# A two-block network in float32 on one core: the residual's second column half transposed without TensorE at two places

## What is computed

```python
for layer in range(DEPTH):                       # DEPTH = 2
    hn = rms_norm(h, mix_norm[layer])
    mixed = rg_lru_block(hn, ...) if layer == 0 else stick_breaking_attention(hn, ...)
    h = h + mixed
    h = h + swiglu_ffn(rms_norm(h, ffn_norm[layer]), ffn_w_in[layer], ffn_w_out[layer])
...
def swiglu_ffn(x, w_in, w_out):                  # 1024 -> 2 x 2816 -> 1024
    gu = jnp.einsum("bsd,df->bsf", x, w_in)
    h = jax.nn.silu(gu[..., :D_FF]) * gu[..., D_FF:]
    return jnp.einsum("bsf,fd->bsd", h, w_out)
```

## Time and profile before

| what | value |
|---|---|
| runs, us | 811.69, 810.04, 811.88 (median 811.69) |
| profiled execution, us | 809.93, of which its span 807.8 |
| PE busy | 802.0 us, 99% of the span |
| PEld busy | 695.2 us, 86% |
| DVE busy | 594.1 us, 74% |
| ACT busy | 533.9 us, 66% |
| POOL busy | 108.7 us, 13% |
| HBM read | 145.94 MB, 184 GB/s over the span with what is written |

### The profile page before, as it was taken

One profiled execution on the slowest core, in us unless ns is written; L12 is line 12 of the kernel. 1 busy time (PEld: TensorE's weight loads), 2 busy tenths in 40 slices (PEclk: granted clock), 3 DMA queues, 4 the chain that ended last, 5 costly groups with the idle time before them and its releaser, 6 DMA issues.

```text
span 807.8 us, 11976 instructions
## 1 busy us (share of the span) xinstructions
PE 802.0 (99%) x4482; PEld 695.2 (86%) x4482; DVE 594.1 (74%) x841; ACT 533.9 (66%) x867; POOL 108.7 (13%) x198
## 2 busy tenths in 40 slices
PE   9999999999999999999999999999999999999998
PEld 8999788888888899887888888888989899888887
DVE  6998886666655579987766666556867689998764
ACT  6887477677656557656766777737664857677432
POOL 0000023444402000000044444202100000000000
PEclk9999999999999999999999999999999999999999
DMA  8964697666565564436676666656464454553511
GB/s 276 324 195 130 224 285 242 198 198 207 186 203 185 157 183 150 143 104 185 209 252 189 183 201 192 192 193 194 159 192 134 154 186 129 173 175 127 184 69 53
DMA packets 119057, 147.79 MB, mean 183 GB/s; under 512 B 7079, under 2 KB 89816, under 8 KB 118872
## 3 DMA queue, kind: packets, MB, share of 16 engines
q1 hardware_dynamic: 117767, 145.43, 57.0%
q10 hardware_dynamic: 1232, 1.59, 0.6%
HBM read 145.94 MB, written 2.63 MB: 184 GB/s over the span
## 4 chain that ended last, share of the span: by engine, by line
PE 98%; DVE 1%; DMA 1%; ACT 0%; issue 0%; SPq 0%; DVEq 0%
PE bank L558 22%; PE bank L560 22%; PE bank L559 22%; PE bank L483 6%; PE bank L484 5%; PE bank L485 5%; PE bank L523 3%; PE bank L525 1%; PE bank L490 1%; PE bank L491 1%; PE bank L492 1%; PE bank L585 1%; PE bank L940 1%; PE bank L817 1%; PE bank L800 1%; DMA const<-in_consts 1%
## 5 line engine op out<-in xcount | busy, mean ns | idle before, releaser
L1728 DVE TENSOR_TENSOR wlo<-raw,whi 128x1024 fp32r<-128x1024 f32 (+1 forms) x268 | 315.9, 1218 | 57.4 <-ACT whi L1141 56.5
L1141 ACT ACTIVATE whi<-raw 128x1024 fp32r<-128x1024 f32 (+1 forms) x260 | 258.5, 1045 | 82.6 <-PE bank L560 60.9
L558 PE MATMUL bank<-whi,xboth 128*128 128x512 f32 x464 | 182.0, 392 | 0.4
L560 PE MATMUL bank<-whi,xboth 128*128 128x512 f32 x464 | 180.7, 389 | 0.0
L559 PE MATMUL bank<-wlo,xboth 128*128 128x512 f32 x464 | 180.6, 389 | 0.0
L1109 POOL COPY xg<-sq 32x128 f32<-32x128 f32 x176 | 96.6, 549 | 381.9 <-DVE sq L2077 375.4
L558 PEld LDWEIGHTS bank<-whi,xboth 128*128 128x128 f32 x464 | 87.1, 188 | 19.0 <-issue 1.1
L560 PEld LDWEIGHTS bank<-whi,xboth 128*128 128x128 f32 x464 | 87.1, 188 | 18.4
L559 PEld LDWEIGHTS bank<-wlo,xboth 128*128 128x128 f32 x464 | 87.1, 188 | 17.7
L483 PE MATMUL bank<-xboth,whi 128*128 128x256 f32 x352 | 100.8, 286 | 0.2 <-DVE wlo L1728 0.2
L485 PE MATMUL bank<-xboth,wlo 128*128 128x256 f32 x352 | 99.6, 283 | 0.0
(11 more groups left out here) (359 smaller groups left out, 1250.0 us busy)
## 6 DMA issues: line engine op xcount, KB each, us to landing
raw<-in_ffn_w_in SPq DMA_DIRECT2D x176, 256.0 KB, 3.6
raw<-in_w_in SPq DMA_DIRECT2D x48, 512.0 KB, 4.5
raw<-in_ffn_w_out SPq DMA_DIRECT2D x44, 512.0 KB, 4.1
raw<-in_attn_w_qkv SPq DMA_DIRECT2D x24, 512.0 KB, 4.6
raw<-in_lru_w_in SPq DMA_DIRECT2D x14, 512.0 KB, 6.5
raw<-in_lru_w_out SPq DMA_DIRECT2D x8, 512.0 KB, 4.3
raw<-in_attn_w_o SPq DMA_DIRECT2D x8, 512.0 KB, 4.8
raw<-in_w_out SPq DMA_DIRECT2D x8, 512.0 KB, 4.3
```

The costliest lines, as they stand in the source:

```text
L558: nc.tensor.matmul(dst, hi, wh, start=start, stop=False)
L560: return nc.tensor.matmul(dst, lo, wh, start=False, stop=stop)
L1141: nc.scalar.activation(whi[:, c % RING, part], raw[:, c % RAWS, part], ACT.Copy).then_inc(hi_done, 1)
L1728: nc.vector.tensor_tensor(wlo[:, c % RING, part], raw[:, c % RAWS, part], whi[:, c % RING, part].bitcast(F32), ALU.subtract).then_inc(lo_d ...
```

## The change

At both places the second column half (j = 2, 3 of norms 1 and 3) is no longer transposed by TensorE. Behind the addition to `h`, VectorE transposes it in 32x32 blocks (`x_turn`), and GpSimd and ScalarE carry the blocks to their partitions with eight copies each (`x_moves`); `norm_hi` and `norm_lo` then read `x_part` in SBUF where they read a PSUM bank. `late_transposes` goes out of `ffn`; it stays in the projections behind norms 2, 4 and 5. The odd norms have buffers of their own (12 and 16 KB into the arena). The tables `XT_BLOCKS` and `XT_BANKS` number the waits, and two increments that stood for transposes that TensorE did not do go away.

```diff
@@ -108,6 +108,13 @@
 X_BANKS = (6, 7, 4, 5)
+
+
+XT_BLOCKS = {(1, 1): 1, (2, 0): 2, (3, 1): 3, (4, 0): 4}
+
+
+XT_BANKS = {key: n + 1 for n, key in enumerate(
+    (xn, j) for xn in range(1, 6) for j in range(4) if (xn, j // 2) not in XT_BLOCKS)}
@@ -200,8 +207,8 @@
-        x_blocks = over("x_blocks", 44, [P, 4, 4, 2, 32])
-        x_part = over("x_part", 48, [P, 4, S])
+        x_blocks = [over(f"x_blocks{n}", kb, [P, 4, 4, 2, 32]) for n, kb in enumerate((44, 12))]
+        x_part = [over(f"x_part{n}", kb, [P, 4, S]) for n, kb in enumerate((48, 16))]
@@ -755,8 +762,6 @@
                     last.then_inc(chunk_done, 1)
-                    if p == 0:
-                        late_transposes(xn, ready, count)
@@ -775,12 +780,9 @@
                     last.then_inc(chunk_done, 1)
-                    if c == 7:
-                        pe.sem_inc(xt_mm, 1)
-                        pe.sem_inc(xt_mm, 1)
@@ -1097,7 +1098,18 @@
         def _(pool):
 
+            def x_moves(xn, half):
+
+                pool.wait_ge(xt_blocks, XT_BLOCKS[xn, half])
+                for i in range(2):
+                    rows = slice(32 * i, 32 * i + 32)
+                    for f in range(4):
+                        dst = x_part[xn % 2][32 * f:32 * f + 32].rearrange("p k (a n) -> p k a n", n=P)
+                        last = nc.gpsimd.tensor_copy(dst[:, :, :, rows], x_blocks[xn % 2][rows, :, f])
+                last.then_inc(xt_pool, 1)
+
             for layer in range(2):
+                x_moves(1 + 2 * layer, 1)
                 for q in range(FFN_PAIRS):
...
-                pool.wait_ge(xt_blocks, layer + 1)
...
+                x_moves(2 + 2 * layer, 0)
@@ -1160,15 +1166,29 @@
+            def x_moves(xn, half):
+
+                act.wait_ge(xt_blocks, XT_BLOCKS[xn, half])
+                for i in range(2, 4):
+                    rows = slice(32 * i, 32 * i + 32)
+                    for f in range(4):
+                        dst = x_part[xn % 2][32 * f:32 * f + 32].rearrange("p k (a n) -> p k a n", n=P)
+                        last = nc.scalar.activation(dst[:, :, :, rows], x_blocks[xn % 2][rows, :, f], ACT.Copy)
+                last.then_inc(xt_act, 1)
+
             def norm_hi(xn, j):
                 if xn == 0 and j == 0:
                     act.wait_ge(first_t, 1)
                 elif xn == 0:
                     act.wait_ge(chunk_done, j + 1)
+                elif (xn, j // 2) in XT_BLOCKS:
+                    act.wait_ge(xt_pool, XT_BLOCKS[xn, j // 2])
+                    act.wait_ge(xt_act, XT_BLOCKS[xn, j // 2])
                 else:
-                    act.wait_ge(xt_mm, 4 * (xn - 1) + j + 1)
-                if xn in (2, 4) and j < 2:
-                    src = [x_part[:, 2 * j:2 * j + 2, :].rearrange("p m n -> p (m n)")] * 2
+                    act.wait_ge(xt_mm, XT_BANKS[xn, j])
+                if (xn, j // 2) in XT_BLOCKS:
+                    k = 2 * (j % 2)
+                    src = [x_part[xn % 2][:, k:k + 2, :].rearrange("p m n -> p (m n)")] * 2
@@ -1359,6 +1379,7 @@
                 norm_square(xn, 0)
                 act.wait_ge(banks_read, b0 + 4 + 4)
                 norm_square(xn, 1)
+                x_moves(xn, 1)
                 norm_hi(xn, 2)
                 norm_hi(xn, 3)
@@ -1822,9 +1836,17 @@
+            def x_turn(xn, half):
+
+                cols = slice(half * WIDE, (half + 1) * WIDE)
+                nc.vector.transpose(x_blocks[xn % 2][:, :, :, :, :].rearrange("p k f a n -> p a (k f) n"),
+                                    h[:, :, cols].rearrange("p a (b n) -> p a b n", n=32)).then_inc(xt_blocks, 1)
+
             def norm_end(name, xn):
 
                 residual_wide(name, 1)
+                dve.wait_ge(banks_read, STAGES[name][2] + 8)
+                x_turn(xn, 1)
                 ahead(STAGES[name][0] + 3)
                 norm_sum(xn)
                 norm_lo(xn, 2)
```

More of the change, by code:

```diff
@@ L737, in _, with ffn @@
             outputs_wide("lru_out", yhi, ylo, y_lo, 1)
-            def ffn(layer, ready, count):
+            def ffn(layer):
                 c0, _, b0 = STAGES[f"ffn_in{layer}"]
@@ L777, in ffn @@
                     last.then_inc(chunk_done, 1)
-                    if c == 7:
-                        pe.sem_inc(xt_mm, 1)
-                        pe.sem_inc(xt_mm, 1)
             pe.wait_ge(p_lo, 1)
-            ffn(0, banks_read, STAGES["lru_out"][2] + 4 + 4)
+            ffn(0)
             c0, _, b0 = STAGES["qkv"]
@@ L852, in _ @@
                         after=4 if g == 1 else 2)
-            c0a, _, b0a = STAGES["attn_out"]
             o_h = ohi[:, :, :].rearrange("p a (b n) -> p (a b) n", n=S)
@@ L861, in _ @@
                           (2, 2): lambda: weight_transposes(GROUPS - 1), (3, 1): lambda: weighted_values(GROUPS - 1)})
-            ffn(1, banks_read, b0a + 4 + 4)
+            ffn(1)
             c0, _, b0 = STAGES["mix_in"]
@@ L1423, in ffn @@
                     if c == 7:
[L1424 to L1430, removed]
+                        x_moves(xn + 1, 0)
                         if layer:
@@ L1435, in ffn @@
                     if c == 8:
-                        act.wait_ge(xt_pool, layer + 1)
-                        act.wait_ge(xt_act, layer + 1)
                         norm_hi(xn + 1, 0)
@@ L2145, in ffn @@
                         dve.wait_ge(acc_read, 4 * layer + 2)
-                        nc.vector.transpose(x_blocks[:, :, :, :, :].rearrange("p k f a n -> p a (k f) n"),
-                                            h[:, :, 0:WIDE].rearrange("p a (b n) -> p a b n", n=32)).then_inc(xt_blocks, 1)
+                        x_turn(xn + 1, 0)
                     if c == 8:
@@ L2260, in final_norm @@
             def final_norm():
-                dve.wait_ge(xt_mm, 16)
+                dve.wait_ge(xt_mm, XT_BANKS[4, 3])
                 for a in range(2):
```

## The result

The changed kernel took 815.8 us as the median of seven executions (814.06 to 817.59); beside it the kernel before had a median of 810.11 (seven executions, lowest 810.02). The ratio is 1.0064 with an interval of 1.0054 to 1.0074: slower, by 0.6%. The profiled execution took 816.06 us, its span is 814.2, and the mean granted clock over it is 0.998.

What follows compares the result with a forecast made beforehand. The prediction took TensorE, busy for 802.0 of 807.8 us, to bound the kernel. Later starts of chunk p = 2, +2.5 and +1.5 us with the transposes' gain included, made +4.0 on a mean of 810.9: 814.9 us, range 811.7 to 817.7.

Steps and rivals of the forecast that it cites:

- The bound: Whole kernel: TensorE sets the time; work taken off it is gained, any wait of it lost in full.
- Step 1: Chunk p = 1: TensorE waits 0.74 us for `wlo` in the first layer, not at all in the second.
- Step 2: Chunk p = 2: starts late behind GpSimd's copies, +2.5 us at the first place, +1.5 at the second.
- What was costed at nothing: Later load into the freed `raw` slot (cover about 7 us), removed `xt_mm` increments, new buffers: no cost.
- Rival 1: Both places: GpSimd's copies are not slowed, ScalarE's end last; +1.8 us in all, 812.7; chance 0.18.
- Rival 2: Chunk p = 2 ready in time at both places, only the gain stays: 1.8 us less, 809.1; chance 0.04.
- Rival 4: The change does nothing at one of the places; given no chance.
- Rival 3: Behind the new waits the clock falls, one chunk per place at 1.2 GHz: 10.9 us more, 825.8; chance 0.05.
- The sum: Both places, gain and p = 1 wait included: +2.5 + 1.5 = +4.0 us, giving 814.9 us; chance 0.70.

Runs made afterwards that it cites:

- four additions: Kernel before, with four unneeded 128x1024 additions on VectorE ahead of `wlo` of chunk p = 2 at both places: 817.75 us, 1.0091.
- three additions: Kernel before, with three unneeded 128x1024 additions on VectorE ahead of `wlo` of chunk p = 2 at both places: 813.22 us, 1.0042.
- filled with matmuls: Changed kernel plus nine unread 128x512 matmuls on TensorE ahead of chunk p = 2 in both layers: 814.05 us, the second time 814.14.
- the three recut ones: Changed kernel recut: half-size copies, second place only, 811.31 us; copies on VectorE and ScalarE, splits around them, ten and six 810.14, eight and eight 809.15.
- eight and eight copies: Changed kernel with GpSimd moving nothing, VectorE and ScalarE eight copies each, splits put around the copies by halves: 809.15 us, 0.9991.

## Why the prediction was right, and where its sum was short

**The bound.** That TensorE's time is the kernel's held: each delay reached the end in full. The two starts of p = 2 are late by 4.2 us in sum, and the executions at full clock are 4.0 and 4.2 us over before.

**Step 1** (p = 1). Forecast: a wait of 0.74 us at the first place and none at the second. Measured: from 100.60 to 101.59 is 0.99, 0.76 over the step of 0.23, and none at the second. The profile names no cause for this wait (`issue`), but the first half of this row of VectorE, the first part of `wlo`, ends at 100.31 + 1.26 = 101.57:

```profile
100.31 2.52 DVE L1741 TENSOR_TENSOR wlo<-raw,whi 128x1024 fp32r<-128x1024 f32 x2
```

**Step 2** (p = 2). Forecast +2.5 and +1.5 us, measured +2.57 and +1.64. The hand-overs, the halves of each split and the order of the engines came out within 0.1 us. The price it rests on, GpSimd's 5.26 us from norm 4, was exact, and so was the reading of it as two long copies: in the changed kernel

```profile
L1108 POOL COPY a_x_part<-a_x_blocks x2: 1297/1298/1300, 100.4 to 101.8; 32x256 f32<-32x256 f32 x2
```

are the two beside `wlo`, and the six behind them took 0.395 us; where the transposition stands behind the subtractions, all eight took 0.392:

```profile
L1108 POOL COPY a_x_part<-a_x_blocks x8: 387/392/398, 104.2 to 107.3; 32x256 f32<-32x256 f32 x8
```

The Trainium skill, in "SBUF — State Buffer" (Who interferes with whom), says that a VectorE instruction with two SBUF inputs contends with a GpSimd instruction that reads SBUF, and calls the shared ports an exclusive lock. The trace agrees: one copy is held for each subtraction, by 0.9 us each.

**What was costed at nothing** stayed at nothing: no other new wait of TensorE is in the list, so the later load into the freed `raw` slot was covered.

**Rival 1** (ScalarE's copies last) fell: ScalarE waited 1.33 us for GpSimd. **Rival 2** (the waits vanish) fell as well; the kernel without copies shows what it would have given, -1.2 us. **Rival 4** fell: both places changed.

**Rival 3 is the step that was mis-sized,** and its own sign, a granted clock under 1.00 behind a gap, is in the profile. It was put as "one chunk of 5.46 us at each place", 10.9 us more, with a chance of 0.05 on the ground that 1.1 us of standing still had left the clock at full. The clock does fall: in 10 of 12 executions of the changed kernel, each with the mean clock of one fall. But it falls for about eight matmuls only, 1.7 us, and then comes back while TensorE works on. A cost of 1.7 us with a high chance was taken for one of 10.9 with a low one. The reason given for the small chance did not carry. The 1.1 us of the earlier trace rows stand ahead of TensorE's very first matmul, which starts at 1.05, so they say nothing of a clock behind work (kernel before):

```profile
1.05 4.63 PE L649 MATMUL bank<-rs 128*128 128x128 f32 x20 [1.05 <-DVE rs L1866]
```

And the length counts: the kernels with waits of up to 1.3 us kept the clock, those with about 2.4 or more lost it in 22 of 30 executions. The page "TensorE: Matmul & The Clock Gate" (HAM oscillation) of the Trainium skill was cited there for the fall; the trace agrees that there is one (0.50 in the windows), not that the whole chunk passes at the lower level.

**The sum.** Forecast +4.0 us, on executions at full clock +4.0 to +4.2, with one fall +5.8. The chain was right, by its mechanism and by its size. The forecast time of 814.9 came 0.9 us short of the 815.8 measured and within its range, and that it came so near is in part luck, since two errors partly cancel: 1.7 us of clock were left out, and the base of 810.9, the mean of four executions, was 0.8 above the 810.1 that the kernel before had as a median beside it. Of the chances, slower by over 0.3% had 0.75.

## What to carry to other kernels

Where one engine is busy for 99% of the span, price a unit of its work by the step between starts there, not by durations, and ask of every operation taken off it how many hand-overs take its place: here 0.9 us of transposes gave way to a chain over three engines that let TensorE stand for 2.4 us. When such an engine begins to stand still, count the clock in as well, and read it in windows of a few us around the gap, since a page of 20 us slices hides a fall of 3 us. If the bounding engine must wait for over 2 us, matmuls that nothing needs can keep the clock up (here 1.7 us), but it is better to shorten the wait: with the copies off GpSimd, the splits put around them and both sets of copies ending together, the kernel became 5 us faster here than the changed one is at full clock.

## What the runs showed of the hardware that was not expected

**The clock's fall behind a wait is partial and not certain.** Executions with a fall among all, by what TensorE did ahead of p = 2:

| kernels | gap between starts, us | executions with mean clock 0.998 or less |
|---|---|---|
| changed (twice), one place only (two kernels), transposition behind, four additions | 2.7 to 4.0 | 22 of 30 |
| three additions | 1.7 | 0 of 5 |
| filled with matmuls (twice) | 0.8, behind the filling | 0 of 10 |
| without copies, the three recut ones | up to 1.7 | 0 of 44 |
| before | none | 0 of 60 |

By kernel: one wait per execution 4 of 10, the changed kernel with its two 10 of 12, the transposition behind (gaps of 4.0 and 3.1 us) 4 of 4, and four additions 4 of 4, though their gaps of 2.8 us are hardly longer than the 2.8 and 2.7 of the changed kernel. Why one execution falls and the next doesn't was not tried; nor is it settled why the changed kernel's two waits never brought two falls in the same execution, where the four additions did in two of four.

**A second spread of 1.8 us lies in the start-up, and the granted clock doesn't show it.** Most kernels, the one before among them, have some executions that are 1.7 to 1.8 us longer at full mean clock (811.69 beside 810.04). The kernel with eight and eight copies was profiled in one (810.58). Matmuls on the line ahead of the program proper, from 6 us on, in it and in the kernel before, busy us and mean ns:

```profile
L657 PE MATMUL bank<-rs 128*128 128x128 f32 x8 | 1.9, 421 | 0.0
```

```profile
L649 PE MATMUL bank<-rs 128*128 128x128 f32 x11 | 1.5, 284 | 0.0
```

The first stand between 7.7 and 9 us, the second between 6 and 7.7; both kernels have a mean of 429 ns until 6, and the granted clock reads 1.00 in both. The first matmul of the program proper starts at 12.46 instead of 10.68, 1.78 us later, and from there on the two run alike. It is there with and without the change, and so it is no part of what the change does; but it does enter where single executions, or medians of few, are compared. What causes it was not tried.
